# Hybrid decoder layer: convolution heads moved ahead of DMAs, two slices moved, and fp32 sums of squares split into fp32r products

## The chip, the core and the metric

The program runs on one core of one Trainium2 chip. The metric is the device time of one execution in microseconds. A core has five engines that matter here: TensorE (PE: matmuls, with its weight loads as PEld), VectorE (DVE), ScalarE (ACT), GpSimd (POOL) and SyncE (SP, which here only issues DMAs). POOL and ACT can issue DMAs too. Each engine runs its own instructions in order and waits on semaphores for the others.

## The reference

One layer of a decoder that runs a stick-breaking attention branch and a Mamba-2 state-space branch side by side, then a SwiGLU block. There are 512 prompt tokens and 8 sequences of 8 new tokens, 576 in all. Cut to what the change touches:

```python
h = rmsnorm(x, p['norm1_w'])
proj = h @ p['w_in']
q, k, v, z, xbc, dt, ga, gb = jnp.split(proj, ...)
q = rmsnorm(q.reshape(b, T, N_Q_HEADS, HEAD_DIM), p['q_norm_w'])   # per head of 64
k = rmsnorm(k.reshape(b, T, N_KV_HEADS, HEAD_DIM), p['k_norm_w'])
...
xbc, conv_new = causal_conv(xbc, conv_state, p['conv_w'], p['conv_b'])  # 4 taps, per channel
xbc = jax.nn.silu(xbc)
xs, Bm, Cm = jnp.split(xbc, ...)
dt = jax.nn.softplus(dt + dt_bias); A = -jnp.exp(a_log)
y, ssm_new = ssd_chunked(xs, dt, A, Bm, Cm, ssm_state)   # chunks of 128 tokens, cumsum of dt*A
```

## The kernel before

All activations lie transposed, channels on the 128 partitions and the 576 tokens along the free axis, in two halves of 288 columns, one PSUM bank each. A projection tile is 128 output channels: `chunk_tile` or `gemm` calls `product` (L487, L488, L491), which for each of eight slices of 128 input channels makes six fp32r matmuls: high part of the weights with high and low part of x, and low part of the weights with the high part of x. A weight chunk is loaded by SP, its high part `w_hi` is made by ACT (`make_hi`, L455) and its low part `w_lo` by DVE (`make_lo`, L461). There are two buffers of each, so the high part of a chunk can be made only when the tile two before it has been multiplied.

The order on each engine is written out by hand. The first stage goes through 13 chunks (`for c in range(N_FIRST)` on TensorE, ACT and DVE): eight of q, two of k, two of v, one of dt. For each of the ten tiles of q and k, DVE copies the tile from PSUM to `pre`, ACT squares it into `sq` (L1813), TensorE sums the squares of each head of 64 with a block matrix of ones (`norm_sums`, L1152: two fp32 matmuls; the profile names that matrix conv_out, whose room it borrows), ACT takes the logarithm and the exponential (`root_of_sums`), DVE scales (`finish_norm`), and ACT and DVE split q into high and low parts (`split_hi`, `split_lo`). The norm sums of tile c-1 stand on TensorE behind the projection of tile c.

After the attention branch and its output projection comes the state-space stage. Its beginning, for group 0, projects six tiles that go through the convolution: B and C (`("bc", 0, 0)`, `("bc", 0, 1)`), then four of x, then a first z tile of which some slices stand around the turns of x (`by_token`, L1436). For each of the six, POOL copies the three old tokens of each sequence into `conv_src` (`conv_head`, L955) and later keeps the new ones (`conv_tail`, L963, L965); ACT copies the tile from PSUM into `conv_src` (L2031 to L2033); DVE convolves (`convolve`, L2570 and three of L2572); ACT applies silu (L2003, L2004). On DVE the low part of the next chunk stands behind the convolution of the tile before. Meanwhile the cumulative sums of dt*A, made by one group of matmuls (L1552) between the first two tiles, go from SBUF to DRAM and back in a layout with one row per head: POOL issues these DMAs (L1015, L1016 out, L995, L998 in, L1006 for the picks).

## Time and profile before

| | us |
|---|---|
| median of 3 runs (lowest, highest) | 1418.91 (1418.65, 1421.53) |
| profiled execution | 1418.91 |
| its span, first to last instruction | 1417.4 |
| mean granted TensorE clock | 0.996 |

| engine | busy us | share |
|---|---|---|
| PE | 1351.2 | 95% |
| PEld | 1257.5 | 89% |
| DVE | 963.0 | 68% |
| ACT | 707.4 | 50% |
| POOL | 263.5 | 19% |

A row of a timeline gives the start of an instruction from the start of the span, its duration (for several in a row the time from the first start to the last end), the engine, the line, the operation, the tile written and the tiles read, and in brackets how long the engine was idle before it and which instruction ended that. Matmuls are pipelined: a row may say 0.29 us for one while the next starts 0.13 us later, so the distance of two starts is what one costs. The granted clock is 1.00 at 2.4 GHz.

### The profile page before, as it was taken

How to read it: one execution, taken by the hardware profiler on the slowest of the kernel's cores; microseconds unless marked ns; L12 is line 12 of the kernel's file. 1: busy time of each engine (PE TensorE's matmuls, PEld its weight loads, DVE VectorE, ACT ScalarE, POOL GpSimd, SP SyncE). 2: the span in 40 equal slices, each digit the busy share in tenths (PEclk: the TensorE clock that was granted, in tenths of full speed). 3: DMA queues.
4: the chain of work that ended last, by engine and by line, in shares of the span. 5: the costliest groups of instructions: out<-in, count | busy, mean ns of one | idle time of the engine just before them, and what ended most of it. 6: DMA issues, size and time to landing. Idle time of an engine off the chain costs nothing. (4 is left out here: it accounts for less than half of the span.)

```text
span 1417.4 us, 26926 instructions
## 1 busy us (share of the span) xinstructions
PE 1351.2 (95%) x10301; PEld 1257.5 (89%) x10301; DVE 963.0 (68%) x1569; ACT 707.4 (50%) x1271; POOL 263.5 (19%) x467
## 2 busy tenths in 40 slices
PE   5999999999999899999999999999999999999996
PEld 4998777899999898888888887899999999999996
DVE  4455546788853476787787776877899999983221
ACT  4576445777632354574464464535644444452221
POOL 4002233000021423333333324211100000000000
PEclk9999999999999999999999999999999999999998
DMA  4226665122255333334334425362333333323331
GB/s 122 75 77 193 180 209 163 56 71 71 71 159 166 75 86 109 95 96 116 107 95 124 109 68 176 111 204 75 90 90 90 104 105 90 90 71 98 97 95 36
DMA packets 200897, 152.86 MB, mean 108 GB/s; under 512 B 15529, under 2 KB 187585, under 8 KB 200720
## 3 DMA queue, kind: packets, MB, share of 16 engines
q1 hardware_dynamic: 175394, 97.93, 24.5%
q0 software_dynamic: 24992, 52.85, 12.7%
q8 instruction: 83, 1.36, 0.4%
q10 hardware_dynamic: 384, 0.37, 0.1%
q14 instruction: 44, 0.35, 0.1%
HBM read 127.80 MB, written 23.29 MB: 107 GB/s over the span
## 5 line engine op out<-in xcount | busy, mean ns | idle before, releaser
L487 PE MATMUL tile_banks<-x_hi,w_hi 128*128 128x288 f32 (+1 forms) x1232 | 368.1, 314 | 11.5 <-DVE w_lo L461 10.1
L488 PE MATMUL tile_banks<-x_lo,w_hi 128*128 128x288 f32 (+1 forms) x1104 | 309.7, 296 | 0.0
L491 PE MATMUL tile_banks<-x_hi,w_lo 128*128 128x288 f32 (+1 forms) x1232 | 262.4, 294 | 0.0
L487 PEld LDWEIGHTS tile_banks<-x_hi,w_hi 128*128 128x128 f32 (+1 forms) x1232 | 231.7, 188 | 25.2 <-DVE w_lo L461 12.4
L461 DVE TENSOR_TENSOR w_lo<-w_raw,w_hi 128x1024 fp32r<-128x1024 f32 (+2 forms) x125 | 150.5, 1204 | 113.0 <-ACT w_hi L455 112.4
L488 PEld LDWEIGHTS tile_banks<-x_lo,w_hi 128*128 128x128 f32 (+1 forms) x1104 | 207.7, 188 | 5.5 <-issue 3.6
L491 PEld LDWEIGHTS tile_banks<-x_hi,w_lo 128*128 128x128 f32 (+1 forms) x1232 | 197.5, 187 | 0.4
L455 ACT ACTIVATE w_hi<-w_raw 128x1024 fp32r<-128x1024 f32 (+2 forms) x125 | 129.5, 1036 | 99.2 <-PE tile_banks L491 94.0
L488 PE MATMUL tile_banks<-f_lo,w_hi 128*128 128x288 f32 x352 | 98.6, 294 | 0.0
L1102 POOL DMA_DIRECT2D out_y_prompt<-y_tok x8 | 6.2, 778 | 386.1 <-ACT y_tok L2315 373.3
L2203 ACT ACTIVATE w_hi<-sum_raw 128x512 fp32r<-128x512 f32 x71 | 44.9, 634 | 60.3 <-PE tile_banks L1674 24.6
L488 PEld LDWEIGHTS tile_banks<-f_lo,w_hi 128*128 128x128 f32 x352 | 66.1, 188 | 0.0
L2572 DVE SCALAR_TENSOR_TENSOR conv_acc<-conv_src,conv_par,conv_acc 128x600 f32<-128x600 f32 x72 | 62.1, 862 | 2.5
L886 POOL DMA_DIRECT2D v_page<-in_cache_v x64 | 34.4, 537 | 154.4 <-issue 154.4
L487 PE MATMUL tile_banks<-y_hi,w_hi 128*128 128x288 f32 x192 | 56.1, 308 | 0.3 <-DVE w_lo L461 0.3
L487 PE MATMUL tile_banks<-t_blocks,w_hi 128*128 128x288 f32 x192 | 54.7, 300 | 1.6 <-DVE f_lo L2931 1.5
L488 PE MATMUL tile_banks<-y_lo,w_hi 128*128 128x288 f32 x192 | 53.8, 295 | 0.0
L2836 DVE TENSOR_TENSOR w_lo<-sum_raw,w_hi 128x512 fp32r<-128x512 f32 x71 | 49.9, 703 | 5.5 <-ACT w_hi L2203 5.5
L2031 ACT ACTIVATE conv_src<-tile_banks 128x288 f32<-128x288 f32 x24 | 9.9, 411 | 87.2 <-PE tile_banks L491 87.2
L2437 DVE TENSOR_TENSOR_SCAN after_w<-rest,zero_col 128x128 f32<-128x128 f32 (+2 forms) x64 | 52.3, 817 | 0.3
L1064 POOL DMA_DIRECT2D out_ssm_sample<-old x32 | 25.5, 797 | 118.1 <-DVE old L2717 108.0
L2439 DVE TENSOR_TENSOR beta<-beta,after_w 128x512 f32<-128x512 f32 (+2 forms) x80 | 42.6, 532 | 2.8
(490 smaller groups left out, 3678.1 us busy)
## 6 DMA issues: line engine op xcount, KB each, us to landing
w_raw<-in_w_in SPq DMA_DIRECT2D x68, 512.0 KB, 4.0
k_page<-in_cache_k SPq DMA_DIRECT2D x64, 128.0 KB, 2.6
v_page<-in_cache_v POOLq DMA_DIRECT2D x64, 128.0 KB, 3.0
old<-in_state_ssm POOLq DMA_DIRECT2D x32, 256.0 KB, 3.5
out_ssm_sample<-old POOLq DMA_DIRECT2D x32, 256.0 KB, 2.9
w_raw<-in_w_pb SPq DMA_DIRECT2D x16, 512.0 KB, 3.5
w_raw<-in_w_down SPq DMA_DIRECT2D x16, 512.0 KB, 4.0
gates_dram<-gate_out POOLq DMA_DIRECT2D x22, 288.0 KB, 2.8
```

What stands on the lines that cost most here:

```text
L455: nc.scalar.activation(w_hi[:, c % 2, 0:tiles, 0:width], w_raw[:, c % 2, 0:tiles, 0:width], ACT.Copy).then_inc(hi_made, 1)
L461: nc.vector.tensor_tensor(w_lo[:, c % 2, 0:tiles, 0:width], w_raw[:, c % 2, 0:tiles, 0:width], f32(w_hi[:, c % 2, 0:tiles, 0:width]), ALU. ...
L487: nc.tensor.matmul(out, wh, xh[:, HALVES[h]], start=start and k == 0, stop=False, skip_group_check=onto)
L488: nc.tensor.matmul(out, wh, xl[:, HALVES[h]], start=False, stop=False, skip_group_check=onto)
L491: mm = nc.tensor.matmul(out, wl, xh[:, HALVES[h]], start=False, stop=stop and k == last, skip_group_check=onto)
L886: eng.dma_start(v_page[:, n % V_SLOTS, :], cache_v[0, bass.ds(page_of(eng, x, k), 1)].rearrange("o p h d -> p (o h d)")).then_inc(sem(f"v_ ...
L1064: eng.dma_start(states_of(ssm_sample, g, b), old[:, b % 2]).then_inc(sem(f"state_stored{b % 2}"), 16)
L2203: eng.activation(form_slot(f)[0], form_raw(f), ACT.Copy).then_inc(sem("form_hi_made"), 1)
L2437: link(eng.tensor_tensor_scan(out=after_w[:, slot, edge - width:edge][:, ::-1], data0=rest[:, slot, cols][:, ::-1], data1=zero_col[:, 0:1] ...
L2439: return eng.tensor_tensor(beta[:, x["u"] % 4, cols], beta[:, x["u"] % 4, cols], after_w[:, slot, edge - width + 1:edge + 1], ALU.mult)
L2572: ins = eng.scalar_tensor_tensor(out=dst, in0=src[:, w:w + m], scalar=conv_par[:, w * CT + ct:w * CT + ct + 1], in1=dst, op0=ALU.mult, op1 ...
L2836: eng.tensor_tensor(low, form_raw(f), f32(high), ALU.subtract).then_inc(sem("form_split"), 1)
```

## The change

There are four edits.

1. The squares of q and k are made twice on ACT, once rounded to fp32r (`sq_hi`) and once in fp32 (`sq`). DVE subtracts them to `sq_lo`. TensorE multiplies both with ones in fp32r (`pair_ones_r`, copied once by ACT), so two fp32 matmuls per tile become four fp32r matmuls. `sq` is no longer double buffered.
2. On POOL the convolution heads of the first two tiles go ahead of the DMAs of the sums, and the tails and the later heads are put between the DMAs that follow.
3. On TensorE six slices of the first z tile, not four, go ahead of the turns of x in group 0; the two between the second and the third turn are gone from there.
4. POOL waits for the picks on `sums_hi_made` instead of `picks_made`; the instruction that signals it is the same.

```diff
-        sq = sb("sq", [P, 2, T], F32, qkv)
+        sq = sb("sq", [P, T], F32, qkv)
+        sq_hi = sb("sq_hi", [P, T], F32R, qkv)
...
+        sq_lo = sb("sq_lo", [P, T], F32R, qkv)
+        pair_ones_r = sb("pair_ones_r", [P, P], F32R, qkv)
...
+            early_keys = group_inputs(0)
+            for key in early_keys[0:2]:
+                conv_head(key)
             eng.wait_ge(sem("sums_split"), 4)
             ...
-            conv_io(group_inputs(0)[0])
+            conv_tail(early_keys[0])
             eng.wait_ge(sem("sums_out"), 16 * 6)
-            for st in range(2):
-                sums_in(st)
-            eng.wait_ge(sem("picks_made"), 1)
+            sums_in(0)
+            conv_tail(early_keys[1])
+            conv_head(early_keys[2])
+            sums_in(1)
+            conv_tail(early_keys[2])
+            conv_head(early_keys[3])
+            eng.wait_ge(sem("sums_hi_made"), 3)
             for g in range(2):
                 picks_in(g)
-            for key in group_inputs(0)[1:]:
-                conv_io(key)
+                conv_tail(early_keys[3 + g])
+                conv_head(early_keys[4 + g])
+            conv_tail(early_keys[5])
...
-                pe.wait_ge(sem("squared"), n + 1)
+                pe.wait_ge(sem("squares_split"), n + 1)
...
-                    pe.matmul(spare(key)[:, 0:HALF], pair_ones[:, :], sq[:, n % 2, HALVES[h]]).then_inc(bank_full[use[key][0]], 1)
+                    pe.matmul(spare(key)[:, 0:HALF], pair_ones_r[:, :], sq_hi[:, HALVES[h]], start=True, stop=False)
+                    pe.matmul(spare(key)[:, 0:HALF], pair_ones_r[:, :], sq_lo[:, HALVES[h]], start=False, stop=True).then_inc(bank_full[use[key][0]], 1)
...
-                    if c in (1, 3, 4):
-                        gemm(key_after, {1: range(4, 6), 3: range(6, 7), 4: range(7, 8)}[c])
+                    if c in parts:
+                        gemm(key_after, parts[c])
...
-            gemm(around, range(0, 4))
+            gemm(around, range(0, 6))
...
+            eng.activation(pair_ones_r[:, :], pair_ones[:, :], ACT.Copy).then_inc(sem("squared"), 1)
...
-                    if c >= 2:
-                        wait_full(eng, ("ss", c - 2, 1))
-                    eng.activation(sq[:, c % 2, :], pre[:, c % 2, :], ACT.Square).then_inc(sem("squared"), 1)
+                    if c >= 1:
+                        wait_full(eng, ("ss", c - 1, 1))
+                    eng.activation(sq_hi[:, :], pre[:, c % 2, :], ACT.Square).then_inc(sem("squared"), 1)
+                    eng.activation(sq[:, :], pre[:, c % 2, :], ACT.Square).then_inc(sem("squared"), 1)
...
-                        eng.wait_ge(sem("squared"), c - 1)
+                        eng.wait_ge(sem("squared"), 2 * (c - 1) + 1)
...
+                if c < KD + 2:
+                    eng.wait_ge(sem("squared"), 2 * (c + 1) + 1)
+                    eng.tensor_tensor(sq_lo[:, :], sq[:, :], f32(sq_hi[:, :]), ALU.subtract).then_inc(sem("squares_split"), 1)
```

How it moves instructions, at three places. First DVE in the first stage, the third tile (c = 2): `pre` is the tile's copy, `normed` the scaled tile before it, `qo` the low parts of q, `w_lo` those of the weights. Before:

```order
L461 TENSOR_TENSOR w_lo<-w_raw,w_hi 128x1024 [waits weights_hi_made]
L2407 COPY pre<-tile_banks 128x576 [waits normed_made,squared,tile_done]
L2378 SCALAR_TENSOR_TENSOR normed<-pre,par,rinv 128x576 [waits rinv_made]
L2389 TENSOR_TENSOR qo<-normed,qo 64x512 [waits qk_hi_made] x2
L461 TENSOR_TENSOR w_lo<-w_raw,w_hi 128x1024 [waits weights_hi_made]
```

and now:

```order
L464 TENSOR_TENSOR w_lo<-w_raw,w_hi 128x1024 [waits weights_hi_made]
L2421 COPY pre<-tile_banks 128x576 [waits normed_made,squared,tile_done]
L2392 SCALAR_TENSOR_TENSOR normed<-pre,par,rinv 128x576 [waits rinv_made]
L2403 TENSOR_TENSOR qo<-normed,qo 64x512 [waits qk_hi_made] x2
L2431 TENSOR_TENSOR sq_lo<-sq,sq_hi 128x576 [waits squared]
L464 TENSOR_TENSOR w_lo<-w_raw,w_hi 128x1024 [waits weights_hi_made]
```

The subtraction `sq_lo` is new and stands between q's low parts and the weights' low part of the next chunk. In the same way ACT's second square stands ahead of q's high parts and of the weights' high part.

Second POOL at the beginning of the state-space stage; L955 (now L958) is a head, L963 and L965 (now L966, L968) a tail. Before:

```order
L1015 DMA sums_dram<-sums 64x128 [waits sums_split]
L1015 DMA sums_dram<-sums 64x128 x3
L1015 DMA sums_dram<-sums 64x64
L1016 DMA minus_dram<-sums 64x576
L955 COPY conv_src<-conv_in 128x8x3
L963 COPY conv_out<-conv_src 128x3 [waits tile_free1,conv_heads]
L965 COPY conv_out<-conv_src 128x24 [waits conv_tail_made]
L995 DMA sum_rows<-sums_dram 8x1x512 [waits sums_out,conv_tails]
L995 DMA sum_rows<-sums_dram 8x1x512
L998 DMA sum_rows<-sums_dram 8x1x512 x2
L995 DMA sum_rows<-sums_dram 8x1x512 x2
L998 DMA sum_rows<-sums_dram 8x1x512 x2
```

and now:

```order
L958 COPY conv_src<-conv_in 128x8x3
L958 COPY conv_src<-conv_in 128x8x3 [waits conv_heads]
L1021 DMA sums_dram<-sums 64x128 [waits sums_split,conv_heads]
L1021 DMA sums_dram<-sums 64x128 x3
L1021 DMA sums_dram<-sums 64x64
L1022 DMA minus_dram<-sums 64x576
L966 COPY conv_out<-conv_src 128x3 [waits tile_free1]
L968 COPY conv_out<-conv_src 128x24 [waits conv_tail_made]
L998 DMA sum_rows<-sums_dram 8x1x512 [waits sums_out,conv_tails]
L998 DMA sum_rows<-sums_dram 8x1x512
L1001 DMA sum_rows<-sums_dram 8x1x512 x2
L966 COPY conv_out<-conv_src 128x3 [waits tile_free0]
```

Two heads have moved ahead of the six DMAs of the sums; tails and heads now stand between those that read them back, and the DMAs of the picks (L1006, now L1009) have moved behind the third tail.

Third TensorE at the turns of x in group 0 (`spare_bank<-ident,xs_t`); the rows on tile_banks are slices of the first z tile. Before:

```order
L1436 MATMUL spare_bank<-ident,xs_t 128x128 x8
L487 MATMUL tile_banks<-x_hi,w_hi 128x288
L488 MATMUL tile_banks<-x_lo,w_hi 128x288
L487 MATMUL tile_banks<-x_hi,w_hi 128x288
L488 MATMUL tile_banks<-x_lo,w_hi 128x288
L491 MATMUL tile_banks<-x_hi,w_lo 128x288 x2
L487 MATMUL tile_banks<-x_hi,w_hi 128x288
L488 MATMUL tile_banks<-x_lo,w_hi 128x288
L487 MATMUL tile_banks<-x_hi,w_hi 128x288
L488 MATMUL tile_banks<-x_lo,w_hi 128x288
L491 MATMUL tile_banks<-x_hi,w_lo 128x288 x2
L1436 MATMUL spare_bank<-ident,xs_t 128x128 x8
```

and now:

```order
L1448 MATMUL spare_bank<-ident,xs_t 128x128 x16
L490 MATMUL tile_banks<-x_hi,w_hi 128x288
L491 MATMUL tile_banks<-x_lo,w_hi 128x288
L490 MATMUL tile_banks<-x_hi,w_hi 128x288
L491 MATMUL tile_banks<-x_lo,w_hi 128x288
L494 MATMUL tile_banks<-x_hi,w_lo 128x288 x2
L1448 MATMUL spare_bank<-ident,xs_t 64x128 x4
```

The two slices that stood between the turns now stand ahead of all of them.

## Rows read from the trace of the kernel before

**Rows 1.** Waits of TensorE, 400 to 600 us: who, for whom, us, times, longest.

```profile
PE tile_banks L487 <- DVE w_lo L461: 7.2, 3, 4.2
...
PE spare_bank L1436 <- ACT xs_t L2004: 1.7, 1, 1.7
```

**Rows 2.** Timeline, TensorE, a q tile: start, us, engine, line, operation, idle before.

```profile
48.62 1.14 PE L1152 MATMUL spare_bank<-sq,conv_out 128*128 128x288 f32 x4
...
55.93 1.14 PE L1152 MATMUL spare_bank<-sq,conv_out 128*128 128x288 f32 x4
...
57.03 0.30 PE L488 MATMUL tile_banks<-x_lo,w_hi 128*128 128x288 f32 x1
```

**Rows 3.** Timeline, DVE, the same tile.

```profile
52.19 1.39 DVE L2389 TENSOR_TENSOR qo<-normed,qo 64x512 fp32r<-64x512 f32 x2 [0.28 <-ACT qo L1783]
...
54.49 1.23 DVE L461 TENSOR_TENSOR w_lo<-w_raw,w_hi 128x1024 fp32r<-128x1024 f32 x1 [0.91 <-ACT w_hi L455]
```

**Rows 4.** Timeline, ACT, the same tile.

```profile
49.31 0.99 ACT L1767 ACTIVATE root<-spare_bank,eps_col 128x288 f32<-128x288 f32 x2 [4.02 <-PE spare_bank L1152]
...
50.97 0.67 ACT L1813 ACTIVATE sq<-pre 128x576 f32<-128x576 f32 x1
...
51.54 1.27 ACT L1783 ACTIVATE qo<-normed 64x512 fp32r<-64x512 f32 x2
...
53.40 1.06 ACT L455 ACTIVATE w_hi<-w_raw 128x1024 fp32r<-128x1024 f32 x1
```

**Rows 5.** Timeline, TensorE, the state-space stage's beginning.

```profile
477.65 0.61 PE L487 MATMUL tile_banks<-x_hi,w_hi 128*128 128x288 f32 x1 [4.21 <-DVE w_lo L461]
...
487.49 0.40 PE L487 MATMUL tile_banks<-x_hi,w_hi 128*128 128x288 f32 x1 [1.94 <-DVE w_lo L461]
487.72 0.29 PE L488 MATMUL tile_banks<-x_lo,w_hi 128*128 128x288 f32 x1
...
512.06 1.09 PE L1436 MATMUL spare_bank<-ident,xs_t 128*128 128x128 f32 x8 [1.73 <-ACT xs_t L2004]
```

**Rows 6.** Timeline, TensorE, the turn of v.

```profile
115.57 0.30 PE L1160 MATMUL spare_bank<-ident,v_t 128*64 128x128 f32 x1 [0.60 <-ACT v_tok L1803]
```

**Rows 7.** Timeline, DVE, the same beginning.

```profile
473.24 0.59 DVE L2570 TENSOR_SCALAR conv_acc<-conv_src,conv_par 128x600 f32<-128x600 f32 x1 [3.80 <-POOL conv_src L955]
...
476.38 1.22 DVE L461 TENSOR_TENSOR w_lo<-w_raw,w_hi 128x1024 fp32r<-128x1024 f32 x1
...
483.06 0.59 DVE L2570 TENSOR_SCALAR conv_acc<-conv_src,conv_par 128x600 f32<-128x600 f32 x1 [5.47 <-POOL conv_src L955]
...
486.21 1.22 DVE L461 TENSOR_TENSOR w_lo<-w_raw,w_hi 128x1024 fp32r<-128x1024 f32 x1
```

**Rows 8.** Timeline, POOL, the same beginning.

```profile
469.74 2.65 POOL L1015 DMA_DIRECT2D sums_dram<-sums  x5 [6.34 <-DVE sums L2558]
...
472.90 0.22 POOL L955 COPY conv_src<-conv_in 128x24 f32<-128x24 f32 x1
...
475.34 1.12 POOL L995 DMA_DIRECT2D sum_rows<-sums_dram  x2 [1.45 <-DMA minus_dram<-sums]
...
482.71 0.24 POOL L955 COPY conv_src<-conv_in 128x24 f32<-128x24 f32 x1
...
486.49 0.99 POOL L963 COPY conv_out<-conv_src 128x3 f32<-128x3 f32 x1 [1.88 <-ACT conv_src L2033]
```

**Rows 9.** Timeline, ACT, the same beginning.

```profile
469.60 0.24 ACT L2033 ACTIVATE conv_src<-tile_banks 128x64 f32<-128x64 f32 x1
...
500.69 0.41 ACT L2031 ACTIVATE conv_src<-tile_banks 128x288 f32<-128x288 f32 x1 [4.07 <-PE tile_banks L491]
...
507.14 0.41 ACT L2031 ACTIVATE conv_src<-tile_banks 128x288 f32<-128x288 f32 x1 [4.07 <-PE tile_banks L491]
...
511.23 0.63 ACT L2003 ACTIVATE xs_t<-conv_acc 128x512 f32<-128x512 f32 x1 [1.71 <-DVE conv_acc L2572]
```

**Rows 10.** Window of x's first tile: busy times, then PEclk, DMA share, GB/s.

```profile
477.65:484.10 6.45, 6.45 (x39) 6.45 (x40) 1.00 (x2) 0.57 (x1) 5.33 (x12) 0.78 0.49 111
```

More of the change, by code:

```diff
@@ L1427, in gemm, with by_token @@
                         mm.then_inc(tile_done, 1)
-            def by_token(g, key_after):
+            def by_token(g, key_after, parts):
                 pe.wait_ge(sem("conv_done"), 6 * (g + 1))
@@ L1558, in _ @@
             around = before_groups[-1]
-            gemm(around, range(0, 4))
+            gemm(around, range(0, 6))
             for g in range(NG):
-                by_token(g, around)
+                by_token(g, around, {1: range(4, 6), 3: range(6, 7), 4: range(7, 8)} if g else {3: range(6, 7), 4: range(7, 8)})
                 plan = ssd_plan(g)
@@ L1995, in _ @@
             eng.activation(pair_picks[used, :].rearrange("p (e d) -> p e d", e=2), pair_rows[used, 0:2].unsqueeze(2).to_broadcast([SEG_ROWS, 2, HD]), ACT.Copy)\
-               .then_inc(sem("picks_made"), 1)
+               .then_inc(sem("sums_hi_made"), 1)
             def conv_silu(key):
```

## The prediction

> **What bounds the kernel now.** The busy times come first: TensorE is busy 95% of the span and every other engine is well below, so the first question at each place is whether TensorE itself gets shorter or waits less. The waits of TensorE in the stretch around the change come second [rows 1]: its projection matmuls waited 7.2 us for the low parts of weights in three places, the longest 4.2 us, and the turns of x waited 1.7 us for ACT's silu. Third, the timeline of one tile of the q, k stage [rows 2]: there TensorE has no wait at all. One tile follows the next every 55.93 - 48.62 = 7.31 us, and the sums of squares (L1152) stand between them. So in the first stage only shorter TensorE work can help, and only as far as ACT and DVE keep up; in the state-space stage a wait can go.
>
> **Sums of squares: what TensorE saves.** From the start of L1152 at 55.93 to the second projection matmul at 57.03, less one steady spacing of 0.13, are 0.97 us [rows 2]: that is the real cost of two fp32 matmuls (four records). The tile's other 7.31 - 0.97 = 6.34 us are 48 fp32r matmuls, 0.132 each. The changed tile has four fp32r matmuls of the same 288 columns: 4 x 0.132 = 0.53. Saved: 0.44 per tile, 4.4 us for ten tiles.
>
> **What ACT and DVE add.** Call E the end of a tile's projection (48.62). The low parts that the next but one tile needs are ready at 54.49 + 1.23 = 55.72, which is E + 7.10 [rows 3]; TensorE wants them at E + 0.97 + 6.34 + 0.97 = E + 8.28. The slack is 1.2 us. The chain to them is ACT's: roots from 49.31, square at 50.97, q's high parts at 51.54, then the weights' high part at 53.40 to 54.46 [rows 4]. The second square adds what the present one takes from start to next start, 51.54 - 50.97 = 0.57. The first half of the sums is ready 0.22 earlier (two passes of 0.132 instead of half of 0.97), so everything behind the roots moves by +0.35. DVE's added subtraction of 576 columns has no row; it lies between nothing and w_lo's 1.23 for 1024 columns, and scaled with the columns is about 0.7. It stands behind q's low parts, which end at 53.58 + 0.35 = E + 5.31, so it ends near E + 6.1, and the weights' high part comes at E + 6.19: it is hidden by a wait that DVE has anyway (0.91 in [rows 3]). If it were a third longer it would start to push w_lo one for one.
>
> The low parts are then ready at E + 7.45, and TensorE wants them at E + 0.53 + 6.34 + 0.53 = E + 7.40. So this wait comes back. With 0.06 from the end of w_lo to the matmul and 0.10 for a restart (487.43 to 487.49, and 0.23 in place of 0.13 to the next matmul [rows 5]) a tile follows the next but one at no less than 6.34 + 7.45 + 0.16 = 13.95 us, against 2 x 6.87 = 13.74 unhindered: 0.10 per tile, for the eight tiles of which the chain holds q's or k's high parts 0.8 us. The norm sums themselves want the new low squares at E + 6.87, 0.8 after they are there. Two one-off terms: the copy of the ones delays the second chunk's w_lo by about 0.1, and the turn of v waits 0.60 for ACT [rows 6]; TensorE comes there 0.44 earlier, ACT only 0.22, so 0.2 is lost. Together: 4.4 - 0.8 - 0.1 - 0.2 = 3.3 us. Bounds: 4.4 if no wait comes, nothing if every tile waits 0.44, and below nothing only if the waits touch the clock (last rival).
>
> **Heads ahead of the sums' transfers.** Why did x's first tile wait 4.21 us [rows 5]? Its w_lo (476.38) is queued on DVE behind the first convolution, which began at 473.24 after 3.80 us of waiting for POOL's head copy [rows 7]; that copy stood at 472.90 behind six transfers of the sums, issued from 469.74 on [rows 8]. With the head done before them, the convolution waits only for ACT's last copy out of PSUM, 469.60 + 0.24 = 469.84 [rows 9], so it starts at about 469.90. It holds DVE for 476.38 - 473.24 = 3.14, w_lo ends at 469.90 + 3.14 + 1.22 = 474.26, and TensorE starts at 474.32, 3.3 us sooner; 0.9 us of the wait stay.
>
> The second convolution now has its head too (it waited 5.47 for it at 483.06), so it runs 474.3 to 477.5 and the next w_lo ends at 478.7. TensorE wants that at 474.32 + 0.1 + 6.45 = 480.87, 6.45 being the distance of two tiles (500.69 to 507.14 [rows 9]). So the wait of 1.94 at 487.49 goes whole. A third piece goes with them: between 477.65 and 487.49 - 1.94 = 485.55 the tile took 7.90, not 6.55, because the granted clock of that stretch was 0.78 [rows 10], partly the lower level of 1.2 GHz, after 4.21 us without a matmul; after the 1.94 us wait the next matmuls came 0.23 and then 0.13 apart, at 2.4 GHz. A wait of 0.9 is nearer to the latter row, so I count the full clock. The sum is 3.33 + 1.94 + 1.35 = 6.6 us, the same as 487.49 - 480.87. If the clock still fell it would be 5.3.
>
> What is late next? The third convolution needs tile 480.87 out of PSUM, about 481.9, and its head. POOL: sums out by 472.9, tail, wait for their landing until 475.34, four transfers (2 x 1.12), tail, head: about 478.6 if copies take 0.2, about 479.9 if they stretch to 0.82 to 0.99 as at 486.49 beside DVE. 2.0 us of slack either way, and another 1.0 before w_lo is late for TensorE. The two picks of the later group move to about 490 and are read near 511; the sums' rows are covered likewise.
>
> **Two more slices ahead of x's turns.** x's last tile ends at 487.49 + 3 x 6.45 = 506.84. Four slices of 6.45/8 = 0.81 followed, then a gap up to 512.06, where ACT's silu of x (511.23 [rows 9]) was done: that is 5.22 after the tile. Six slices take 4.84, so about 0.4 of gap is left, and the two slices that stood between the turns are gone from there: 1.6 us. The turns then run four deep; the fifth needs the bank that DVE reads first, long free. DVE's scaling of x comes out about 0.9 earlier, but the matmuls behind it are gated by B's turns, so I take 1.6; the bounds are nothing and the gap itself, 2.0.
>
> **Sum.** 3.3 + 6.6 + 1.6 = 11.5 us. The profiled execution took 1418.91 us (span 1417.4 and 1.5 around it), which is also the median of the three runs. Forecast: 1407.4 us.
>
> **Rivals.**
> *A, the split gives nothing:* each tile waits for w_lo as long as its sums got shorter (a DVE subtraction of 1.2 instead of 0.7 would do). For it: the margin on DVE is 0.1 us. Against: the nearest rows scale to 0.7. 1407.4 + 3.3 = 1410.7.
>
> *B, POOL stays late:* the six transfers now run beside a convolution, and the later heads are queued behind transfers and tails. If each issue and copy of POOL is held up by DVE until DVE falls idle at 478.7, the sums go out 6 x 0.53 later at 481.9, land 2.4 after, four transfers and the tail and head reach 488.3, and the third convolution starts 6.4 late; 1.0 is covered, 5.4 is lost: 1412.8. For it: a copy took 0.99 at 486.49, beside DVE. Against: transfers took 1.12 a pair at 475.34, beside DVE's w_lo at 476.38, no more than elsewhere; it decides from 3.0 us of delay on.
> The Trainium skill (SBUF — State Buffer, Who interferes with whom) makes this a rule: a vector instruction in a two-port mode takes the port pair that it shares with GpSimd whole, and a DMA issued by GpSimd can't write its descriptors until it ends. By that rule the convolution's TENSOR_SCALAR could block, its three following instructions with two SBUF inputs only GpSimd's reads. The stretched copies agree with it, and no run here shows a blocked issue.
>
> *C, later stages take it back:* everything behind the first stage comes 3.3 us earlier and meets transfers that do not depend on TensorE. Against: page and weight loads wait for tiles and follow it. Half of the first stage's gain and of the turns' would go: 1409.9.
>
> *D, no wait in the first stage:* w_lo in time because a start or a square is shorter by 0.1: 1406.5.
>
> *E, slower:* the short waits, one per tile, bring the lower clock. A tile at 1.2 GHz takes 6.34 more; eight of them 51 us, 1458. It decides from 2.3 such tiles on (11.5 + 2.8, over 6.34). Against: after 1.94 idle the clock stayed [rows 5], and these waits are 0.2 us in 14.
>
> **How the numbers follow.** Forecast 0.60, A 0.12, B 0.09, C 0.09, D 0.08, E 0.01, and 0.01 that nothing is measured. My own case reaches from 1406 to 1409. With A, C and D inside, 1404.8 to 1411.2 leaves B, E and the tails outside. A measurement of this kernel tells 0.2%, 2.8 us, from no change: faster 0.97, same 0.02, slower 0.01.
>
> **What would show it.** Right: four records for the sums of squares in about 0.53 us; tiles 6.9 to 7.0 apart with a short wait for w_lo before most; the first convolution at about 470 minus 3.3; one wait of 0.9 in place of 4.2 before x's first tile, none before the second, and 0.4 before the turns. Wrong: tiles still 7.3 apart; a convolution that waits for a head; a granted clock below 1 in the first stage; or the turns' fifth step waiting for DVE.

## The result and the profile after

| | before | changed kernel |
|---|---|---|
| median, us (lowest, highest) | 1418.85 (1418.65, 1421.53; 4 runs) | 1405.69 (1404.72, 1406.12; 4 runs) |
| profiled execution, us | 1418.91 | 1405.4 |
| its span | 1417.4 | 1403.9 |
| mean granted clock | 0.996 | 0.996 |

The ratio is 0.9904, 95% interval 0.9891 to 0.9917: 13.2 us less in the medians, 13.5 in the profiled spans, against 11.5 forecast. Two later comparisons of the same kernel gave 0.9919 and 0.9914, so their mean, about 12.4 us, is the better figure of the gain. One execution each of e4_two_heads and e7_sq_lo_twice below, and one of the kernel before, took 1863 to 3137 us; every median and ratio here leaves them out.

Where did it come from? The starts of the same TensorE instructions, in both traces:

| start of | before | after | gained so far |
|---|---|---|---|
| first turn of v (end of the first stage) | 114.4 | 110.8 | 3.6 |
| prompt part of the attention | 238.0 | 233.6 | 4.4 |
| cumulative sums of dt*A | 465.6 | 461.5 | 4.1 |
| turns of x | 512.1 | 501.3 | 10.8 |
| segment sums | 519.3 | 506.9 | 12.4 |
| end of the sums of y's squares, state-space stage | 915.6 | 903.0 | 12.6 |
| first product of the SwiGLU block (`form`) | 1009.6 | 995.8 | 13.8 |
| last turn, at the kernel's end | 1407.9 | 1394.4 | 13.5 |

The stretch from the cumulative sums to the segment sums holds the order of POOL and the slices. It took 53.7 us before and takes 45.4 now.

TensorE at a q tile, from the timeline of the changed kernel, which answers to [rows 2] (start, us, line, operation; in brackets the idle time before):

```profile
48.36 0.29 PE L1163 MATMUL spare_bank<-sq_hi,pair_ones_r 128*128 128x288 f32 x1
48.49 0.29 PE L1164 MATMUL spare_bank<-sq_lo,pair_ones_r 128*128 128x288 f32 x1
48.62 0.30 PE L1163 MATMUL spare_bank<-sq_hi,pair_ones_r 128*128 128x288 f32 x1
48.75 0.29 PE L1164 MATMUL spare_bank<-sq_lo,pair_ones_r 128*128 128x288 f32 x1
...
55.22 0.29 PE L1163 MATMUL spare_bank<-sq_hi,pair_ones_r 128*128 128x288 f32 x1
...
55.76 0.40 PE L490 MATMUL tile_banks<-x_hi,w_hi 128*128 128x288 f32 x1
56.00 0.29 PE L491 MATMUL tile_banks<-x_lo,w_hi 128*128 128x288 f32 x1
...
62.31 0.29 PE L1163 MATMUL spare_bank<-sq_hi,pair_ones_r 128*128 128x288 f32 x1
```

The four products take 0.52 us where two fp32 ones took 0.97. One tile takes 55.22 - 48.36 = 6.86, the next 62.31 - 55.22 = 7.09: the tile behind 55.22 has a short restart at 55.76, 0.24 to the next start in place of 0.13, and so has about every second tile. DVE and ACT at the same tile, which answer to [rows 3, 4]:

```profile
52.18 1.39 DVE L2403 TENSOR_TENSOR qo<-normed,qo 64x512 fp32r<-64x512 f32 x2 [0.85 <-ACT qo L1795]
53.60 0.76 DVE L2431 TENSOR_TENSOR sq_lo<-sq,sq_hi 128x576 fp32r<-128x576 f32 x1
54.48 1.23 DVE L464 TENSOR_TENSOR w_lo<-w_raw,w_hi 128x1024 fp32r<-128x1024 f32 x1
```

```profile
50.38 0.67 ACT L1826 ACTIVATE sq_hi<-pre 128x576 fp32r<-128x576 f32 x1
50.96 0.67 ACT L1827 ACTIVATE sq<-pre 128x576 f32<-128x576 f32 x1
51.53 1.27 ACT L1795 ACTIVATE qo<-normed 64x512 fp32r<-64x512 f32 x2
...
53.39 1.06 ACT L458 ACTIVATE w_hi<-w_raw 128x1024 fp32r<-128x1024 f32 x1
```

The low parts of the weights end at 54.48 + 1.23 = 55.71, 0.05 before TensorE's 55.76: the chain that had 1.2 us of slack has none left. `sq_lo` fills the wait that DVE had before `w_lo`; it ends at 54.36 and ACT's `w_hi` at 54.45, 0.12 and 0.03 before `w_lo` starts.

The beginning of the state-space stage: TensorE's waits for `w_lo` from 400 to 600 us (who, for whom, us, times, longest), to be held against [rows 1]; then DVE and POOL, which answer to [rows 7, 8].

```profile
PE tile_banks L490 <- DVE w_lo L464: 2.2, 2, 1.3
```

```profile
465.80 0.59 DVE L2587 TENSOR_SCALAR conv_acc<-conv_src,conv_par 128x600 f32<-128x600 f32 x1 [0.42 <-ACT conv_src L2047]
466.43 2.60 DVE L2589 SCALAR_TENSOR_TENSOR conv_acc<-conv_src,conv_par,conv_acc 128x600 f32<-128x600 f32 x3
468.94 1.22 DVE L464 TENSOR_TENSOR w_lo<-w_raw,w_hi 128x1024 fp32r<-128x1024 f32 x1
470.23 0.59 DVE L2587 TENSOR_SCALAR conv_acc<-conv_src,conv_par 128x600 f32<-128x600 f32 x1
...
477.79 0.59 DVE L2587 TENSOR_SCALAR conv_acc<-conv_src,conv_par 128x600 f32<-128x600 f32 x1 [3.19 <-ACT conv_src L2047]
```

```profile
465.93 2.66 POOL L1021 DMA_DIRECT2D sums_dram<-sums  x5 [6.12 <-DVE sums L2575]
468.58 0.54 POOL L1022 DMA_DIRECT2D minus_dram<-sums  x1
469.12 1.09 POOL L966 COPY conv_out<-conv_src 128x3 f32<-128x3 f32 x1
...
474.96 0.21 POOL L958 COPY conv_src<-conv_in 128x24 f32<-128x24 f32 x1
475.47 1.07 POOL L998 DMA_DIRECT2D sum_rows<-sums_dram  x2 [0.29 <-POOL conv_src L958]
```

No convolution waits for POOL any more: each is released by ACT's copy or not at all. The third head (474.96) is done at 475.17, 2.6 us before the third convolution (477.79) wants it. TensorE in the same stretch, which answers to [rows 5], and the granted clock of x's first tile, which answers to [rows 10]:

```profile
470.22 0.40 PE L490 MATMUL tile_banks<-x_hi,w_hi 128*128 128x288 f32 x1 [0.84 <-DVE w_lo L464]
...
501.25 1.97 PE L1448 MATMUL spare_bank<-ident,xs_t 128*128 128x128 f32 x16
...
506.88 0.50 PE L1485 MATMUL spare_bank<-sum_rows,picks_even 16*128 16x512 f32 x2
```

```profile
470.22:476.67 6.45, 6.45 (x48) 6.45 (x49) 4.26 (x5) 3.01 (x4) 4.92 (x11) 1.00 0.52 127
```

The 4.21 us have become 0.84, the 1.94 are gone, and the clock of the tile is 1.00 where it was 0.78.

### The profile page after: what moved, and what is told of

Its sections match the earlier page's. It is cut to its first block and busy times, and to the rows that moved or that the text cites. A ratio compares the mean times of both kernels' runs of the same rounds, so it can differ in the third digit from the quotient of the medians.

```text
span 1403.9 us, 26945 instructions
## 1 busy us (share of the span) xinstructions
PE 1348.2 (96%) x10301; PEld 1256.6 (90%) x10301; DVE 970.3 (69%) x1579; ACT 712.5 (51%) x1282; POOL 264.1 (19%) x467
## 5 line engine op out<-in xcount | busy, mean ns | idle before, releaser
L2217 ACT ACTIVATE w_hi<-sum_raw 128x512 fp32r<-128x512 f32 x71 | 44.9, 634 | 59.9 <-PE spare_bank L1686 22.0
```

The costliest lines, as they stand in the source:

```text
L2217: eng.activation(form_slot(f)[0], form_raw(f), ACT.Copy).then_inc(sem("form_hi_made"), 1)
```

## The experiments

Each kernel was timed against the kernel before on the chip that it ran on. The first four change the kernel before, the others the changed kernel. Gains below are (1 - ratio) x 1418.

| kernel | median, us | ratio, 95% interval | gain |
|---|---|---|---|
| e1_split | 1415.10 | 0.9980 [0.997, 0.999] | 2.8 |
| e2_heads | 1411.57 | 0.9952 [0.9938, 0.9965] | 6.8 |
| e3_slices | 1417.26 | 0.9988 [0.9979, 0.9997] | 1.7 |
| e4_two_heads | 1412.10 | 0.9961 [0.9948, 0.9974] | 5.5 |
| e5_after_again | 1406.71 | 0.9919 [0.9902, 0.9936] | 11.5 |
| e6_dve_square | 1405.93 | 0.9916 [0.9898, 0.9934] | 11.9 |
| e7_sq_lo_twice | 1407.29 | 0.9933 [0.9912, 0.9955] | 9.5 |
| e8_conv_first | 1404.69 | 0.9906 [0.9890, 0.9922] | 13.3 |
| e9_best | 1404.71 | 0.9898 [0.9883, 0.9914] | 14.5 |
| e10_seven | 1405.25 | 0.9901 [0.9886, 0.9916] | 14.0 |
| e11_after_third | 1406.53 | 0.9914 [0.9900, 0.9929] | 12.2 |
| e12_first_and_seven | 1404.39 | 0.9897 [0.9881, 0.9914] | 14.6 |

The intervals reach 1.3 to 3 us to either side, so smaller differences are read from the traces, one profiled execution of each kernel. One thing has to be known for that. In the stretch of x's tiles the same tile of 48 matmuls takes one of three durations, 6.45, 6.32 or 6.24 us, the same for the x tiles of an execution, at a granted clock of 1.00 (the first x tile behind a wait of 4.2 us takes longer), and changing from one execution to another on one chip. So the length of the stretch from the cumulative sums to the segment sums, in us below, is compared between executions of the same tile time:

| tile | kernels of the old POOL order | heads moved | changed kernel and its variants |
|---|---|---|---|
| 6.45 | before 53.7 | | changed 45.4, e6 45.3, e8 44.6, e9 44.2, e12 44.2 |
| 6.32 | e1 53.3, e3 51.7 | e2 46.4, e4 47.7 | e5 44.8, e11 44.9 |
| 6.24 | | | e7 44.5, e10 44.0 |

### The three parts alone

**e1_split**: the changed kernel with POOL's order and the slices put back, so that only this is new:

```diff
-                    pe.matmul(spare(key)[:, 0:HALF], pair_ones[:, :], sq[:, n % 2, HALVES[h]])
+                    pe.matmul(spare(key)[:, 0:HALF], pair_ones_r[:, :], sq_hi[:, HALVES[h]], start=True, stop=False)
+                    pe.matmul(spare(key)[:, 0:HALF], pair_ones_r[:, :], sq_lo[:, HALVES[h]], start=False, stop=True)
```

> The kernel before with only the split of the squares into two fp32r products (and the semaphore of the picks merged). My theory: TensorE saves 0.44 us per tile on the sums, a short wait for w_lo comes back on the tiles whose chain holds q's high parts, 3.5 us are gained by the end of the first stage; if page loads give nothing more the time is 1415.4, and if the 0.6 to 0.9 us that the changed kernel's trace showed behind that stage (TensorE waited less for k_page) come from an earlier start as well, 1414.6. Rival A (the wait eats all of it): 1418.9.

**e2_heads**: the kernel before with POOL's new order alone:

```diff
+            for key in early_keys[0:2]:
+                conv_head(key)
             ...
-            conv_io(group_inputs(0)[0])
+            conv_tail(early_keys[0])
             ...
+            conv_head(early_keys[2])
```

> The kernel before with only POOL's new order (heads ahead of the sums' transfers, tails and heads between the later ones). My theory: 3.3 us of TensorE's wait, the second wait of 1.9 and 1.35 us at the lower clock go, 6.6 in all: 1412.2, and x's first tile runs at the full clock. If the lower clock cost nothing or stays, 5.3: 1413.6. If the gain of the changed kernel came mostly from elsewhere, above 1414.

**e3_slices**: the kernel before with the slices alone:

```diff
-            gemm(around, range(0, 4))
+            gemm(around, range(0, 6))
-                by_token(g, around)
+                by_token(g, around, {1: range(4, 6), 3: range(6, 7), 4: range(7, 8)} if g else {3: range(6, 7), 4: range(7, 8)})
```

> The kernel before with only six slices, not four, ahead of the turns of x in group 0. My theory: the gap before the turns shrinks from 2.0 to 0.4 us and nothing is late behind it: 1417.2. Rival: DVE's scaling of x, which comes out only 0.9 earlier, gates the matmuls behind it: 1418.0 to 1418.9.

Measured: 2.8, 6.8 and 1.7 us, together 11.3, within their errors the 11.5 to 13.6 of all three (the gains of the changed kernel's three comparisons). Each in its place: the split took the nine tile distances of the first stage from 65.76 us (41.31 to 107.07) to 62.24 (41.23 to 103.47). The heads took 53.3 - 46.4 = 6.9 us out of the stretch, the slices 53.3 - 51.7 = 1.6, both at a tile of 6.32.

TensorE's waits at the beginning, first with the split alone, then with the heads alone (timelines):

```profile
473.04 0.61 PE L490 MATMUL tile_banks<-x_hi,w_hi 128*128 128x288 f32 x1 [4.15 <-DVE w_lo L464]
...
482.88 0.40 PE L490 MATMUL tile_banks<-x_hi,w_hi 128*128 128x288 f32 x1 [1.03 <-DVE w_lo L464]
```

```profile
474.07 0.40 PE L487 MATMUL tile_banks<-x_hi,w_hi 128*128 128x288 f32 x1 [0.77 <-DVE w_lo L461]
```

The split does nothing for these waits, the heads alone remove them. The first pair teaches one thing more: the two rows stand 482.88 - 473.04 = 9.84 us apart, as in the kernel before (487.49 - 477.65), while the second wait is 1.03 and not 1.94. The tile between was slower and the wait shorter by the same amount. The second convolution sets the second row, so the clock that fell in the first tile cost nothing by itself there: it hid in the wait behind it. In the sum it is right to count both, because both go; it would have been wrong to price the clock as a gain beside a wait that stays.

The slices alone show no gain at the end of their profile (the last turn at 1408.2, before 1407.9). That execution was the slowest of the twelve of this kernel (1419.24 us, median 1417.26), and its trace shows where the 1.9 us that it had at the segment sums went: 0.8 into a longer wait at the first out-projection tile, 2.2 us where the kernel before has 1.4, and 1.5 into the clock behind that wait. The wait in a listing of waits (who, for whom, us, times, longest), DVE's row that TensorE waits for, and the window of that tile (the last three numbers are the granted clock, the DMA share and GB/s):

```profile
PE tile_banks L487 <- DVE conv_acc L2804: 2.2, 1, 2.2
```

```profile
944.98 0.76 DVE L2812 TENSOR_TENSOR conv_acc<-conv_acc,conv_src 128x576 f32<-128x576 f32 x1 [1.65 <-DMA conv_src<-gates_dram]
```

```profile
951.74:958.19 6.45, 6.45 (x37) 6.45 (x38) 6.02 (x8) 2.92 (x5) 0.00 (x0) 0.74 0.29 83
```

DVE waits there for a gate that is read back from DRAM. The same wait of TensorE is 1.4 before, 1.5, 1.4 and 1.4 in e1, e2 and e4, and 0.6, 1.3 and 1.6 in three executions of the changed kernel, which has the slices too. So it changes by 1 us with nothing changed. The 2.2 is above all of these, and one trace can't show whether the slices have a part in it; the ratio over twelve executions, 1.7 us, says that most of them kept the gain.

### How many heads

**e4_two_heads**: the kernel before; the heads of the first two tiles go ahead of the sums' transfers, all the rest of POOL's order stays.

```diff
+            for key in group_inputs(0)[0:2]:
+                conv_head(key)
             ...
-            conv_io(group_inputs(0)[0])
+            conv_tail(group_inputs(0)[0])
             ...
-            for key in group_inputs(0)[1:]:
+            conv_tail(group_inputs(0)[1])
+            for key in group_inputs(0)[2:]:
                 conv_io(key)
```

> The kernel before with the first two heads ahead of the sums' transfers and all the rest of POOL's order as it was. If the two heads are all that matters: 1412.2, as with the whole new order. My theory says that the third head is late then: behind sums, picks and the second tail it is done at about 484 to 485 (on the clock of the trace of before) where the third convolution wants it at 481.9; 1.0 us is covered, 1.5 to 2 are lost: 1414.0, with a wait for w_lo before x's third tile.

Measured: 5.5 us, 1.3 less than with the full order, and in the traces 47.7 - 46.4 = 1.3 us more between sums and segment sums. POOL's timeline and DVE's:

```profile
479.86 1.07 POOL L1006 DMA_DIRECT2D picks_odd<-minus_dram  x2 [0.93 <-issue]
...
481.44 0.21 POOL L955 COPY conv_src<-conv_in 128x24 f32<-128x24 f32 x1
```

```profile
481.75 0.59 DVE L2573 TENSOR_SCALAR conv_acc<-conv_src,conv_par 128x600 f32<-128x600 f32 x1 [5.16 <-issue]
```

The third head comes at 481.44, behind eight transfers in, four of the picks and the second tail, and the third convolution right behind it. ACT's copies were out at 479.6, so it is late by 2 us, of which 1.3 reach TensorE. The interleaving of tails and heads between the transfers is worth these 1.3 us; the two early heads are worth the other 5.5. The expectation had put the loss at 1.5 to 2.

### The first stage's margin

**e5_after_again**: the changed kernel itself.

> The changed kernel once more, beside the three variants of it that follow, so that they stand against it on one chip. The three parts alone gave 3.0 us (split), 6.5 (order of GpSimd) and 0.8 (slices), together 10.3; the changed kernel gave 13.2. If the parts simply add and the rest was the drift between jobs, it is now nearer 1407.5; if they help one another (a transfer that feeds the first out-projection tile comes in time in the one and not in the other), 1405 to 1406 again, and the wait of that tile for its convolution near 945 us is again under 1 us where the slices alone had 2.2.

Measured: 1406.71 us, 11.5 us under the kernel before, and the wait near 945 us is 1.3. The second alternative falls with that wait; the parts add, as far as intervals of 1.3 to 2.4 us can tell.

**e6_dve_square**: the fp32 square on DVE (ACT keeps only `sq_hi`):

```diff
-                    eng.activation(sq[:, :], pre[:, c % 2, :], ACT.Square)
+                    link(eng.tensor_tensor(sq[:, :], pre[:, c % 2, :], pre[:, c % 2, :], ALU.mult))
```

> The changed kernel, with the fp32 square that the split starts from made on VectorE (one multiplication into the same tile) and no longer on ScalarE. Theory: in the first stage the small matmuls of a tile wait for w_lo, at the end of a chain ScalarE root, two squares, two copies to the split; without the second square (0.57 us) the chain is shorter than TensorE's own work, the short wait goes in all ten tiles, and tiles stand 6.86 us apart always; 0.10 to 0.24 us a tile, 0.5 to 1.5 us in all, about 1404.8. Rival: VectorE's own row sets w_lo, so its added multiplication (about 0.5 us) is paid in the small matmuls of each of the eight waiting tiles: 3 to 4 us slower than the changed kernel, 1409.

**e7_sq_lo_twice**: DVE's subtraction twice:

```diff
+                    link(eng.tensor_tensor(sq_lo[:, :], sq[:, :], f32(sq_hi[:, :]), ALU.subtract))
                     eng.tensor_tensor(sq_lo[:, :], sq[:, :], f32(sq_hi[:, :]), ALU.subtract)
```

> The changed kernel with the subtraction that makes the second part of the squares issued twice on VectorE (0.76 us more a tile, the same values). It prices the slack behind that instruction. Theory (the changed kernel's trace: VectorE goes from it to w_lo with about 0.1 us between): w_lo comes 0.65 to 0.76 us later in each tile, the small matmuls wait as long, and the ten tiles lose 4 to 7 us: 1409.5 to 1412.5, with waits for w_lo of 0.8 us a tile. This is the rival in which the split of the squares gives nothing, had VectorE been slower. Rival: the work of the next tile is taken into the gap, and only half is lost, 1408.

Starts of L1163 (first of the four products) in TensorE's timeline, first with the square on DVE, then with the subtraction twice, and there also DVE's `w_lo` before the first wait:

```profile
48.24 0.29 PE L1163 MATMUL spare_bank<-sq_hi,pair_ones_r 128*128 128x288 f32 x1
...
55.10 0.29 PE L1163 MATMUL spare_bank<-sq_hi,pair_ones_r 128*128 128x288 f32 x1
...
103.12 0.29 PE L1163 MATMUL spare_bank<-sq_hi,pair_ones_r 128*128 128x288 f32 x1
```

```profile
54.27 0.39 PE L1163 MATMUL spare_bank<-sq_hi,pair_ones_r 128*128 128x288 f32 x1
...
55.39 0.40 PE L490 MATMUL tile_banks<-x_hi,w_hi 128*128 128x288 f32 x1 [0.33 <-DVE w_lo L464]
...
61.83 0.30 PE L1163 MATMUL spare_bank<-sq_hi,pair_ones_r 128*128 128x288 f32 x1
...
68.70 0.39 PE L1163 MATMUL spare_bank<-sq_hi,pair_ones_r 128*128 128x288 f32 x1
```

```profile
54.12 1.22 DVE L464 TENSOR_TENSOR w_lo<-w_raw,w_hi 128x1024 fp32r<-128x1024 f32 x1
```

With the square on DVE all tiles are 6.86 apart: nothing waits, and this is TensorE's own time. Nine distances take 61.74 us, 0.7 less than in the changed kernel (62.42); the ratios give 0.4 us over e5, too little to be told apart. The theory holds for the place; at the end of the kernel 0.7 us remain within the noise.

With the subtraction twice, two tiles take 68.70 - 54.27 = 14.43 us where the changed kernel needs 13.95, and the nine distances 64.45 where it needs 62.42. So 0.76 us more on DVE in each of two tiles cost 0.24 a tile, 2.0 us in the first stage and 2.0 us in the ratios (11.5 to 9.5). That is under the 4 to 7 us that I expected; the rival was nearer.

Only every second tile waits (55.39, 69.83 and so on), and the rows say why. Count from E, the end of a tile's projection, which is where L1163 starts. Before the first wait E is 47.41, and `w_lo` is ready at 54.12 + 1.22 = 55.34, E + 7.93, where TensorE could take it at E + 7.40: it waits. That wait stands behind the next E (54.27), so the next chain starts unhindered, but TensorE comes to its end half a microsecond later: `w_lo` is ready at 62.30, the four products behind 61.83 end at 62.36, and nothing waits. What the chain is late by is thus paid once in a pair. It is the prediction's own bound for two tiles, 6.34 + 7.93 + 0.16 = 14.43; I had not used it when I expected a loss in each tile.

### What is left at the beginning

**e8_conv_first**: ACT's copy of the first convolution's operand and DVE's first convolution ahead of the copy and the split of the sums. The lines only change places, ACT's making of the picks with them:

```diff
-                wait_full(eng, ("sums", n))
-                eng.activation(sums[:, cols], spare(("sums", n))[:, 0:m], ACT.Copy).then_inc(sem("sums_hi_made"), 1)
             ...
+                wait_full(eng, ("sums", n))
+                eng.activation(sums[:, cols], spare(("sums", n))[:, 0:m], ACT.Copy).then_inc(sem("sums_hi_made"), 1)
             ...
-                eng.wait_ge(sem("sums_hi_made"), n + 1)
-                ...
-                    eng.tensor_tensor(sums[rows, cols], spare(key)[rows, 0:m], f32(sums[rows, cols]), ALU.subtract).then_inc(sem("sums_split"), 1)
             ...
+                eng.wait_ge(sem("sums_hi_made"), n + 1)
+                ...
+                    eng.tensor_tensor(sums[rows, cols], spare(key)[rows, 0:m], f32(sums[rows, cols]), ALU.subtract).then_inc(sem("sums_split"), 1)
```

> The changed kernel, with ScalarE's copy of the first convolution's operand and VectorE's first convolution put ahead of the copy and split of the sums (and of the picked sums). Theory: the wait of 0.84 us before x's first tile is VectorE's first convolution, which starts only when the sums are split and the operand is copied; started about 2 us earlier, the wait goes whole: -0.8 us, 1404.8. Rival: the sums' transfers, which now leave up to 3 us later, make the picks and the mask late (VectorE's xdt and cb_m before x's turns), and the gap before the turns grows by more than the 0.8: 1406 to 1408.

Measured: 44.6 against 45.4 us at a tile of 6.45, 0.8 less, as expected. In TensorE's timeline x's first tile starts without a wait:

```profile
468.76 0.40 PE L490 MATMUL tile_banks<-x_hi,w_hi 128*128 128x288 f32 x1
```

That is 7.9 us after the cumulative sums, 8.7 in the changed kernel. The sums' transfers leave later, and nothing behind them was late. The theory holds; the ratios give 1.8 us against e5 with intervals that overlap, and the traces explain 0.8 of it.

**e10_seven** (with **e11_after_third** beside it): one more slice ahead of the turns.

```diff
-            gemm(around, range(0, 6))
+            gemm(around, range(0, 7))
-                by_token(g, around, {1: range(4, 6), 3: range(6, 7), 4: range(7, 8)} if g else {3: range(6, 7), 4: range(7, 8)})
+                by_token(g, around, {1: range(4, 6), 3: range(6, 7), 4: range(7, 8)} if g else {4: range(7, 8)})
```

> The changed kernel with seven slices of the next tile ahead of x's turns, not six, which asks whether the number of slices is right. Theory: a gap of 0.4 us stands before the turns with six slices (0.8 us each), so a seventh ends it and no more: -0.4 at the first of the segment sums. Rival: no gap is left in the changed kernel, and the seventh slice only makes the turns and all that needs x later by 0.8 us: the segment sums start 0 to 0.8 us later, and the end with them, 1406.5.

> The changed kernel once more, beside the two variants of it in these runs. 1405.69 and 1406.71 us so far: 1405 to 1407, 11.5 to 13.5 us under the kernel before.

The last product before the turns of x, the turns, and the turns of B behind them (`bc_t`) in TensorE's timeline, with six slices (e7, which has the changed kernel's order here and e10's tile time) and then with seven (e10):

```profile
500.20 0.42 PE L494 MATMUL tile_banks<-x_hi,w_lo 128*128 128x288 f32 x2
500.89 1.97 PE L1448 MATMUL spare_bank<-ident,xs_t 128*128 128x128 f32 x16 [0.28 <-ACT xs_t L2018]
...
504.73 0.60 PE L1456 MATMUL spare_bank<-ident,bc_t 128*128 128x128 f32 x4
```

```profile
500.17 0.42 PE L494 MATMUL tile_banks<-x_hi,w_lo 128*128 128x288 f32 x2
500.43 2.34 PE L1448 MATMUL spare_bank<-ident,xs_t 128*128 128x128 f32 x20
...
503.41 0.60 PE L1456 MATMUL spare_bank<-ident,bc_t 128*128 128x128 f32 x4
```

With six slices a gap stands before the turns: 0.69 us from the start of the last pair of products to the turns, where 0.26 is the undisturbed distance, so 0.43 are lost (the idle time of 0.28 is less, since it counts from a modelled end). With seven it is gone, and all twenty turns run in one piece; from the turns to B's turns are 2.98 us in place of 3.84, which is the moved slice (6.24/8 = 0.78) and 0.08 more. The two, 0.43 and 0.08, are the whole difference of the stretch, 44.0 against 44.5 us. The theory gave 0.4, the rival 0 to 0.8 later; the rival falls. e11 came to 1406.53, inside its range, with a gap of 0.40 (idle 0.22).

**e9_best** has all three extras, **e12_first_and_seven** the two of the beginning.

> The changed kernel with three things more: the fp32 square on VectorE (alone it took the first stage's tiles from 6.94 to 6.86 us apart), the first convolution ahead of the split of the sums (alone, sums to x's turns took 38.9 us where the changed kernel takes 39.3 to 39.8), and a seventh slice of the next tile ahead of x's turns. Theory: they lie in three places of TensorE's row, one after the other, and add: 0.8 + 0.6 + 0.4 of the remaining gap before the turns' results are used, 1404 in the median against 1405.7 to 1406.7 for the changed kernel. Rival: from the turns on, TensorE's later work waits for VectorE and ScalarE, which started no earlier, and only the first stage's 0.8 is left at the end: 1405.5.

> The changed kernel with two of the three extras: the first convolution ahead of the split of the sums, and the seventh slice; the fp32 square stays on ScalarE. With all three, the segment sums started 2.3 us earlier than in the changed kernel but 1.1 us were then lost in a wait for the old state's transfer, and the end came 1.0 us earlier. Theory: that transfer's wait is set by how early the stage begins, so with the beginning 0.8 us later than in the kernel of all three the wait is 0 to 0.5 us, and the end comes at the same time: 1404.5 in the median. Rival: the wait of 1.1 was that one execution's, and this kernel, with less taken out, is 0.7 us slower than the one of all three: 1405.3.

They have the lowest ratios, some 2 us under the changed kernel (14.5 and 14.6 us gained, against 11.5 to 13.6). The intervals of the ratios still overlap. The end of e9 lies between its theory (1404) and its rival (1405.5), and decides neither. The third extra, the square on DVE, adds nothing that the ratios show. One wait behind the stage took some of it; waits of TensorE from 500 to 905 us, of e9 and then of e12:

```profile
PE spare_bank L1532 <- DMA old<-in_state_ssm: 1.1, 1, 1.1
```

```profile
PE spare_bank L1532 <- DMA old<-in_state_ssm: 0.5, 1, 0.5
```

The turn of the old state waits for its load from memory: not at all in e5 and e8, 0.3 us in e10, e11 and the changed kernel's first profile, 0.5 in e12, 1.1 in e9. In e9 the stage starts earliest (segment sums at 504.3), which fits a load that is late next. But e8 started at 505.4 without such a wait, e12 at 506.6 with 0.5, and the kernel before, which starts latest of all (519.3), has 1.0. So the wait does not follow the early start, and the theory of e12, that it does, is not borne out, though its time (1404.4, forecast 1404.5) is.

## Why the prediction was right, point by point

- **TensorE's saving in the squares.** 0.97 to 0.52 us a tile, as worked out (0.53).
- **The chain on ACT and DVE.** The second square added 50.96 to 51.53, 0.57 us; `sq_lo` took 0.76 where "about 0.7" was scaled from `w_lo`. The pair of tiles shown takes 13.95 us, forecast 13.95, but there is luck in so close a match: `w_lo` was ready 7.35 us after the tile's projection, not 7.45 (the two roots took 0.89 us in place of 0.99), which by the prediction's formula gives 13.85. Of the 0.23 by which the longer tile exceeds 6.86, 0.11 are the restart and 0.02 a delay before it; the other 0.1 stand nowhere as a wait, and their cause is open. The nine distances gained 3.34 us; 0.44 a tile less 0.8 for the chain gives 3.2. e6 shows that the chain's part is real (6.86 throughout when the square is taken off it), e7 that the formula holds where the chain is clearly late.
- **The turn of v.** Its wait for ACT grew by 0.11, from 0.60 to 0.71; 0.2 had been forecast.
- **Heads.** 4.21 to 0.84 (0.9 forecast), the wait of 1.94 gone, the granted clock of the tile 0.78 to 1.00, the third head long in time. Alone 6.9 us in the trace and 6.8 in the ratio, forecast 6.6.
- **Slices.** 1.6 us alone in the trace at like tile time, forecast 1.6. The gap of 0.4 that was to stay was 0.29 in the changed kernel's first profile and 0.40 in e5 and e11, by the distance of the starts (the profile's idle time shows 0, 0.22 and 0.22).
- **Together** the stretch from sums to segment sums went from 53.7 to 45.4: 8.3 us, forecast 6.6 + 1.6 = 8.2.
- **Rivals.** *A, the split gives nothing*: falls with e1 (2.8 us). *B, POOL stays late*: falls. The five transfers of the sums, now beside a convolution, took 2.66 us, as before without one (2.65 [rows 8]). The Trainium skill (SBUF — State Buffer, Who interferes with whom) would let a vector instruction in a two-port mode hold up such issues. The one candidate, the TENSOR_SCALAR at 465.80, ran when they began at 465.93, and none was seen to be held. They did begin 2.59 us after the start of DVE's split, where it had been 2.34, but in e8 it is 2.59 too, and there the TENSOR_SCALAR was long over. The same section lets GpSimd's reads contend with a vector instruction that has two SBUF inputs, and with that the trace agrees: a copy of three columns took 1.09 us at 469.12, beside DVE's `w_lo`, and 0.18 at 477.81, beside a TENSOR_SCALAR. (The pair of transfers at 475.34 that the prediction puts beside `w_lo` ran almost wholly before it; the next pair, at 476.42, was the one beside it and took 1.10.) *C, later stages take it back*: falls; behind the stage the gain grew, from 12.4 to 13.5, in e5 from 12.5 to 13.0. *D, no wait in the first stage*: its condition came, `w_lo` 0.1 sooner, and yet the tiles were no shorter than forecast; e6, with 0.57 taken off the chain, is what D would have been. (1407.4 less its 0.8 is 1406.6, not 1406.5.) *E, the clock*: falls for the first stage, whose granted clock is 1.00 from 35 to 112 us.
- **What was missed: 1 to 2 us.** 11.5 us stand in the sum. The profiled execution gained 13.5, the medians 13.2, the three comparisons on average 12.4, and the parts alone add to 11.3; what is missing over the average, 0.9, is less than the interval of any one comparison. In the first profile 0.3 more than forecast came in the first stage (3.6) and 0.8 in the attention behind it, where waits for the pages of keys were 4.0 us before and 3.1 here (3.8 and 3.4 in e5 and e11). Later the wait for the old state was 0.7 shorter (1.0 and 0.3) and the one at the first out-projection tile 0.8 (1.4 and 0.6; 1.3 and 1.6 in e5 and e11). These waits change from execution to execution of one kernel, so they look like chance and not like a term that the sum lacks. One thing went the other way: at the beginning of the SwiGLU block TensorE waited 2.19 us in one piece, in the kernel before 0.88 and 1.33, and the granted clock of the 3.2 us behind it was 0.50. So the forecast's 11.5 is nearer to the average than the first result makes it look.

## What to carry to other kernels

A wait of TensorE for a weight's low part was neither about the weight nor about the engine that makes it: it stood two queues back, in a 0.2 us copy behind 3 us of DMA issues on an idle engine. Follow such a wait through every in-order queue until an instruction was free to run but stood behind another, and move that one. Where a cheaper form adds work to helper engines, compute when the next operand is ready and when it is wanted, both from the same origin: here the two were 0.05 us apart, and about 0.1 us a tile came back. What such a chain is late by is paid once in two tiles where the wait stands behind the point from which the next chain starts. And compare stretches between executions only where an unchanged piece inside them takes the same time.

## What the runs showed of the hardware that was not expected

- The same x tile of 48 fp32r matmuls takes 6.24, 6.32 or 6.45 us in an execution, all at a granted clock of 1.00; one kernel had 6.45 in one execution and 6.32 in two others. In the first stage such a tile with its four small products took 6.86 unhindered in all of them (6.77 in a few tiles). What sets it I don't know; it moves the end by up to 1 us in this stretch.
- After 4.15 to 4.22 us without a matmul the next stood 0.24 us apart and the granted clock of the following 6.45 us was 0.61 (e1), 0.74 (e3) and 0.78 (before); after 0.84, 1.03, 1.44, 1.70 and 1.94 us it stayed at 1.00. In between it went both ways: after 2.23 us (e3, 951.74) it fell to 0.74 over a tile, after 2.19 us at the beginning of the SwiGLU block it fell in the changed kernel's first profile, in e9 and in e10, and after the same 2.19 us in e11 it stayed. So a wait of 2.2 us can cost more than itself: in e3 0.8 us of longer wait came with 1.5 us of slower matmuls.
- Lengthening the producer of `w_lo` by 0.76 us in each tile cost 0.24 a tile, and only every second tile waited.
